# Odd mixer: pooled products around the gate matmuls, square roots two units later, forward scan into the kept sum, convolution ahead of the backward scan

## The reference, cut to what matters

```python
def odd_mixer(h, hc, w_in, pool_w, pool_scale, conv_w, conv_b, wa, ba, wx, bx, lam, need_ctx):
    z = h @ w_in
    ux, ug, up = jnp.split(z, CD_SPLITS, axis=-1)
    zc = hc @ w_in[:, :LRU_W]
    xl = depthwise_conv(ux, conv_w, conv_b, LRU_PAD)
    xc = depthwise_conv(zc[..., :LRU_W], conv_w, conv_b, LRU_PAD)
    h_lat = 0
    for d, reverse in enumerate((False, True)):
        # rglru_coeffs: r = sigmoid(u@wa + ba), gi = sigmoid(u@wx + bx), log_a = c * r
        #               a = exp(log_a), b = sqrt(1 - a^2) * gi * u
        a_c, b_c = rglru_coeffs(xc, wa[d], ba[d], wx[d], bx[d], lam[d])
        hs_c = linear_scan(a_c, b_c, 0, reverse)
        a_l, b_l = rglru_coeffs(xl, wa[d], ba[d], wx[d], bx[d], lam[d])
        h_lat = h_lat + linear_scan(a_l, b_l, hs_c[:, 0] if reverse else hs_c[:, -1], reverse)
    return [multiscale_pool(up, pool_w, pool_scale), h_lat * jax.nn.gelu(ug)]
```

## Time and profile before

| | us |
|---|---|
| median of 3 runs | 2664.08 |
| lowest, highest | 2663.63, 2664.1 |
| the profiled execution | 2664.78 |
| its span, first to last instruction | 2662.7 |
| TensorE busy in it | 2267.3 (85%) |
| odd mixer's units in the span, from L1873's first start to its last end | 1585.6 to 1848.5 |

### The profile page before, as it was taken

The page is one execution under the profiler, slowest core; times in us unless marked ns, Lnnn a source line. Parts: engine busy times, 40 slices in busy tenths (PEclk is TensorE's granted clock), DMA queues, the critical chain, the costliest instruction groups (busy, mean ns, idle before and its releaser), DMA issues. The chain is left out here.

```text
span 2662.7 us, 35013 instructions
## 1 busy us (share of the span) xinstructions
PE 2267.3 (85%) x15264; PEld 1086.8 (41%) x15264; DVE 729.2 (27%) x1158; ACT 607.1 (23%) x916; POOL 175.2 (7%) x126
## 2 busy tenths in 40 slices
PE   6498998987995699999999639888984999998874
PEld 3277886554443233333333224444433233332223
DVE  0422324653015211111111373444224111111104
ACT  2421012551004111111111143554013111111102
POOL 0001000000000000000000202241000000000002
PEclk8589999997997799999999759998996999999996
DMA  9600105305421889889999320001003999999985
GB/s 376 224 24 16 40 24 203 122 1 189 152 101 42 335 356 416 355 350 412 415 415 414 126 85 24 24 17 70 0 3 145 409 409 420 415 425 414 426 359 196
DMA packets 139500, 595.85 MB, mean 224 GB/s; under 512 B 25332, under 2 KB 52688, under 8 KB 114640
## 3 DMA queue, kind: packets, MB, share of 16 engines
q1 hardware_dynamic: 111824, 524.86, 49.3%
q0 software_dynamic: 11952, 43.52, 4.4%
q10 hardware_dynamic: 15568, 25.17, 2.7%
HBM read 534.79 MB, written 58.72 MB: 223 GB/s over the span
## 5 line engine op out<-in xcount | busy, mean ns | idle before, releaser
L1548 PE MATMUL ph<-w,x_t 128*32 128x512 f32 x6016 | 681.4, 606 | 39.9 <-DMA w<-in_exp_w 37.7
L1548 PEld LDWEIGHTS ph<-w,x_t 128*32 128x32 f32 x6016 | 190.5, 112 | 453.3 <-issue 428.4
L1561 PE MATMUL py<-w,g_t 128*32 128x512 f32 x3008 | 341.1, 594 | 1.0 <-DVE g_t L1667 1.0
L1661 DVE TENSOR_TENSOR hidden<-hidden,ph 64x512 f32<-64x512 f32 x94 | 101.9, 1084 | 768.4 <-ACT hidden L1619 768.4
L1166 PE MATMUL z<-Y,w_o 128*128 128x512 f32 (+1 forms) x640 | 255.5, 556 | 0.0
L1619 ACT ACTIVATE hidden<-ph 64x512 f32<-64x512 f32 x94 | 55.6, 592 | 695.7 <-PE ph L1548 695.7
L1873 PE MATMUL z<-hT,w_cd 128*128 128x512 f32 (+1 forms) x448 | 192.8, 590 | 4.9 <-ACT hT L477 4.9
L1561 PEld LDWEIGHTS py<-w,g_t 128*32 128x32 f32 x3008 | 93.6, 110 | 205.0 <-issue 203.7
L691 PE MATMUL z<-h_high,w_hi 128*128 128x512 f32 (+1 forms) x432 | 161.7, 374 | 15.3 <-DVE h_low L525 15.3
L1166 PEld LDWEIGHTS z<-Y,w_o 128*128 128x128 f32 x640 | 120.6, 192 | 128.7 <-issue 125.1
L1526 POOL DMA_INDIRECT x_rows<-h_tokens,index x47 | 44.4, 945 | 1843.0 <-PE px L1533 996.2
(11 more groups left out here) (293 smaller groups left out, 2104.0 us busy)
## 6 DMA issues: line engine op xcount, KB each, us to landing
w<-in_exp_w SPq DMA_DIRECT2D x192, 2048.0 KB, 15.7
ada_raw<-in_ada_w SPq DMA_DIRECT2D x24, 2048.0 KB, 17.9
y_slots<-y_rows ACTq DMA_DIRECT2D x188, 128.0 KB, 8.9
y_slots<-zero SPq DMA_DIRECT2D x29, 512.0 KB, 15.3
h_tokens<-h_rows SPq DMA_DIRECT2D x18, 512.0 KB, 2.6
w_ab<-in_w_in_ab SPq DMA_DIRECT2D x14, 512.0 KB, 3.9
w_cd<-in_w_in_cd SPq DMA_DIRECT2D x12, 512.0 KB, 3.9
x_t_saved<-xT SPq DMA_DIRECT2D x8, 640.0 KB, 8.1
```

What stands on the lines that cost most here:

```text
L1548: ins = pe.matmul(ph[row:row + UNIT, :], xt[:, k, at:at + UNIT], w13[:, place[2 * b + n] % RING, half, k, :], start=(k == 0), stop=(k == K ...
L1561: ins = pe.matmul(py[b % 2][row:row + UNIT, :], gt[:, k, n * UNIT:(n + 1) * UNIT], w2[:, place[2 * b + n] % RING, k, half * 512:(half + 1) ...
L1661: dve.tensor_tensor(hid[PAIR:P, :].rearrange("s (k q) -> s q k", k=FT), hid[0:PAIR, :].rearrange("s (q k) -> s q k", k=FT), ph[PAIR:P, :]. ...
```

## The change

It leaves every computation as it is and moves or redirects these:

1. **Pooled products.** Both now stand at one unit, ux i+1 c = 2 (for round 3: ug1 c = 0). After that unit's matmuls TensorE does the first pooled product, into the other bank (that of the unit before), then the second gates (rounds 0 to 2), then the second pooled product into this unit's bank. ScalarE scales both out directly after its copy of that unit.
2. **Second gates** after ux i+1 c = 2 instead of c = 1 (round 3: as before).
3. **Square roots** later: direction 0 at ux i+1 c = 1 instead of c = 0 (round 3: ug0 c = 1), direction 1 at up i+1 c = 1 instead of c = 0 (round 3: ug2 c = 0).
4. **Forward scan** over the latent tokens writes straight into `total[i]` and signals `s_fwd`; the sum adds the backward scan to it in place. `gate_out` of direction 0 waits for `s_fwd` in place of `s_sum`.
5. **Sigmoids**: `pxg` (into G) first, then `pa`; GpSimd's product waits for the first of them alone.
6. **Convolution** of round i ahead of `under_root` of the last round's direction 1.

```diff
             gates_at[place["up", i, 1]] = (i, 0)
-            gates_at[place["ux", i + 1, 1] if later else place["ug", 0, 1]] = (i, 1)
-            roots_at[place["ux", i + 1, 0] if later else place["ug", 0, 0]] = (i, 0)
-            roots_at[place["up", i + 1, 0] if later else place["ug", 1, 0]] = (i, 1)
-            for c in range(2):
-                pool_at[place["ux", i + 1, 1 + c] if later else place["ug", 1, c]] = (i, c)
+            gates_at[place["ux", i + 1, 2] if later else place["ug", 0, 1]] = (i, 1)
+            roots_at[place["ux", i + 1, 1] if later else place["ug", 0, 1]] = (i, 0)
+            roots_at[place["up", i + 1, 1] if later else place["ug", 2, 0]] = (i, 1)
+            n = place["ux", i + 1, 2] if later else place["ug", 1, 0]
+            pool_at[n] = i
+            pool_in[n - 1], pool_in[n] = 2 * i, 2 * i + 1
...
                     ins.then_inc(s_z, 1)
+                    if n in pool_at:
+                        pool_product(pool_at[n], 0, n - 1)
                     if n in gates_at:
                         gates(*gates_at[n])
                     if n in pool_at:
-                        pool_product(*pool_at[n], n)
+                        pool_product(pool_at[n], 1, n)
...
                     if i:
-                        act.wait_ge(s_sum, i)
-                    for gate, (dst, ps, name) in enumerate(((R, pa, "lru_ba"), (G, pxg, "lru_bx"))):
+                        act.wait_ge(s_sum if d else s_fwd, i)
+                    for gate, (dst, ps, name) in enumerate(((G, pxg, "lru_bx"), (R, pa, "lru_ba"))):
...
                     if n in pool_at:
-                        pool_out(*pool_at[n], n)
+                        pool_out(pool_at[n], 0, n - 1)
+                        pool_out(pool_at[n], 1, n)
...
-                    link.step(dve.tensor_tensor_scan(flip(G[:, lat]), flip(R[:, lat]), flip(S[:, lat]), first,
-                                                     ALU.mult, ALU.add))
+                    if d == 0:
+                        dve.tensor_tensor_scan(total[i], R[:, lat], S[:, lat], first, ALU.mult, ALU.add).then_inc(s_fwd, 1)
+                    else:
+                        link.step(dve.tensor_tensor_scan(flip(G[:, lat]), flip(R[:, lat]), flip(S[:, lat]), first,
+                                                         ALU.mult, ALU.add))
...
-                    dve.tensor_tensor(total[i], lanes[0][1][:, 0:SEQ], lanes[1][1][:, 0:SEQ], ALU.add).then_inc(s_sum, 1)
+                    dve.wait_ge(s_fwd, i + 1)
+                    dve.tensor_tensor(total[i], total[i], lanes[1][1][:, 0:SEQ], ALU.add).then_inc(s_sum, 1)
...
+                    conv(i)
                     if i:
                         under_root(i - 1, 1)
-                    conv(i)
-                    if i:
                         scans(i - 1, 1)
...
-                        pool.wait_ge(s_r, 2 * k + 2)
+                        pool.wait_ge(s_r, 2 * k + 1)
```

More of the change, by code:

```diff
@@ L1769, in odd_mixer @@
         place = {(kind, i, c): n for n, (m, i, kind, c) in enumerate(unit)}
-        gates_at, roots_at, pool_at = {}, {}, {}
+        gates_at, roots_at, pool_at, pool_in = {}, {}, {}, {}
         for i in range(BR):
@@ L1797, in odd_mixer @@
             s_w = [self.sem(ctx, f"o_w{i}") for i in range(NW)]
-            (s_sum, s_gw, s_pw, s_zero, s_z, s_ux, s_ug, s_up, s_cv, s_pg, s_r, s_a, s_q, s_sq, s_b, s_h, s_gu, s_y, s_pl, s_pd,
+            (s_sum, s_fwd, s_gw, s_pw, s_zero, s_z, s_ux, s_ug, s_up, s_cv, s_pg, s_r, s_a, s_q, s_sq, s_b, s_h, s_gu, s_y, s_pl, s_pd,
              s_pm, s_pe, s_ch) = (
-                self.sem(ctx, "o_" + n) for n in ("sum", "gw", "pw", "zero", "z", "ux", "ug", "up", "cv", "pg", "r", "a", "q", "sqr",
+                self.sem(ctx, "o_" + n) for n in ("sum", "fwd", "gw", "pw", "zero", "z", "ux", "ug", "up", "cv", "pg", "r", "a", "q", "sqr",
                                                   "b", "h", "gu", "y", "pl", "pd", "pm", "pe", "ch"))
@@ L1813, in wait_z_read @@
                     eng.wait_ge({"ug": s_ug, "up": s_up}[kind], 2 * i + c + 1)
-                if n in pool_at:
-                    of, half = pool_at[n]
-                    eng.wait_ge(s_pe, 2 * of + half + 1)
+                if n in pool_in:
+                    eng.wait_ge(s_pe, pool_in[n] + 1)
             @block.sync
```

## The result

The changed kernel's median is 2638.82 us (four runs, 2635.5 to 2642.04) beside 2663.86 for the kernel before (2661.9 to 2664.1): ratio 0.9908, 95% interval 0.989 to 0.9925, or 25.0 us. The forecast was 2643.5, 20.8 us saved by its sum. The profiled execution is the slowest of the four, 2642.04, with a span of 2640.0 (before: 2662.7).

What follows compares the result with a forecast made beforehand. TensorE, busy 85% of the span, was taken to bound the kernel, with 37.5 us lost in the odd mixer; 10.6 of waits and 6.1 of clock stay, so 20.8 saved: 2643.3, say 2643.5 us, range 2634 to 2651.

Steps and rivals of the forecast that it cites:

- The budget: TensorE in the odd mixer: 37.5 us lost above its work, 24.5 idle ahead of pooled products, 13.0 slow matmuls after waits.
- The copy's wait goes: Second pooled product, rounds 0 to 2: the 16.9 us of waits for ScalarE's copy and their clock cost go away.
- The convolution's room: Ahead of the next round's first gates: convolution needs 13.1 us, TensorE has 14.6 of work, so 1.5 us clear, no cost.
- GpSimd by turns: Pooling: GpSimd and VectorE wait for each other's instructions, so TensorE waits 4.0 us in round 1 and 4.7 in round 2.
- rival by form: GpSimd's later passes take 3.05 us whatever VectorE does; waits 0.1 and 3.6, 28.5 us saved, 2635.6 us; chance 0.18.
- rival without collision: GpSimd's and VectorE's turns fall otherwise: no wait in rounds 1 and 2, 2.6 to 4 us left, 2630; chance 0.07.
- Round 2's wait: TensorE waits 4.7 us for GpSimd's pooling ahead of the second gates, with one pass more than round 1.
- round 3's: Waits ahead of round 3's two pooled products, for GpSimd (0.5 us) and for the copy of ug1 c = 0: together 1.9.
- Round 1's wait: TensorE waits 4.0 us for GpSimd's pooling ahead of the second gates, with the subtraction done at 25.4 us.
- Clock: Slow matmuls behind waits: 2.7 us each in rounds 1 and 2 (2.4 to 3.0), 0.7 in round 3; 6.1 in all.
- In sum: Mixer: 10.6 us of waits and 6.1 of clock stay, 16.7 against 37.5, so 20.8 us saved.
- The rule on the shared ports: Whole-instruction lock: VectorE's product in round 2 would wait for GpSimd's scaling, some 1.6 us more, 2645.

Runs made afterwards that it cites:

- the fastest kernel: Changed kernel with both pooled products behind the second gates and round 3's products one unit later, at ug1 c = 1: mixer 190.8 us, median 2627.4 us.
- the convolution second: Changed kernel with the convolution put back behind under_root of the last round's direction 1: mixer 214.3 us, median 2652.6 us, ratio 0.9934 to 0.9965.
- the places alone: Kernel before with only the new places of pooled products and second gates: mixer 221.2 us, median 2659.4 us, ratio 0.998 to 1.0002.
- short under_root: Changed kernel with VectorE's two under_root instructions writing 8 columns, not 1283 (values wrong): mixer 197.3 us, median 2634.9 us.
- sigmoids as before: Changed kernel with the sigmoid of R first and GpSimd's product after both sigmoids: mixer 208.0 us, median 2647.3 us, ratio 0.9924 to 0.9951.
- forward scan as before: Changed kernel with the forward scan into the lane and the first sigmoid behind the sum again: mixer 214.0 us, median 2653.2 us.
- roots as before: Changed kernel with the square roots at their old units: mixer 202.9 us, median 2641.3 us, ratio 0.9903 to 0.994.

## Why the prediction was right, point by point

- **The budget.** 37.5 us of losses, 24.5 in waits: the fastest kernel has won 35.7 of it.
- **The copy's wait goes.** As told. The copy of the 256-token unit started 0.18 us after the root and 0.2 after the unit's end, in round 0 of both traces of the changed kernel.
- **The convolution's room.** 1.5 forecast, 1.2 measured. The two kernels with `under_root` ahead show what it is worth: waits of 4.39 us (the convolution second) and 4.46 (the places alone) in each of three rounds.
- **GpSimd by turns.** Right, and the step that decides: product 4.57 (4.8 forecast), sum 3.75 (3.8), a wait in round 1 and in round 2, none in round 0. The rival by form is refuted by short under_root; the rival without collision by the 4.57.
- **Round 2's wait** was 4.68 against 4.7, **round 3's** 1.68 against 1.9.
- **Round 1's wait was mis-sized**: 2.26 against 4.0. The step was the last turn. I let VectorE's product, released by the root at 21.5, go ahead of the subtraction and hold it until 23.0. GpSimd was 0.6 us faster through the passes and scaling than I had it, its subtraction began at 1682.96, and VectorE's product at 1683.08: 0.12 us decided that VectorE waited (3.57 for 1.50) and not GpSimd. In the edit with the sigmoids as before VectorE's product was 0.09 us ahead (1684.59 and 1684.68), GpSimd's edges lost 1.6 us to it, and the wait was 4.68.
- **Clock was mis-sized**: 1.8 us behind each of the two long waits, where I took 2.7 (range 2.4 to 3.0), and about 0.2 in round 3, where I took 0.7. The same kernel again had 1.8 and 2.3. My range came from the waits of 6.29 and 3.89 us. The trace of before had a third, of 4.33 us in round 2, near in length to the 4.68, and behind it product and units cost 1.8 us (1761.23 to 1777.60, 16.37 for 14.59):

```profile
1761.23 1.14 PE L1859 MATMUL z<-pool,pool_weights 128*128 128x512 f32 x2 [4.33 <-ACT u_pad L1930]
1762.17 15.59 PE L1873 MATMUL z<-hT,w_cd 128*128 128x512 f32 x32
1777.60 2.31 PE L1848 MATMUL pa<-x_conv,gate_w 128*128 128x512 f32 x6
```

- **In sum** 16.7 us were to stay and 13.2 did: 1.7 from round 1's turn, 1.8 from the clock behind the long waits, the rest from small terms that cancel. The mixer won 24.4 us, the medians 25.0.
- **The rule on the shared ports.** The Trainium skill, SBUF — State Buffer, "Who interferes with whom", has the engine that issues first hold the ports that VectorE and GpSimd share for its whole instruction. The traces agree for two-input instructions (4.57, 3.75, 3.57) and not for GpSimd's scaling. In round 2 of the changed kernel VectorE's product ran its solo 1.50 in the middle of it; VectorE's timeline:

```profile
1728.54 1.50 DVE L1983 TENSOR_TENSOR lru<-lru 128x1283 f32<-128x1283 f32 x1 [3.38 <-ACT lru L1920]
```

GpSimd's scaling there is 1727.02 to 1729.79, in the fence above. By the rule the product would have waited 1.2 us for it. The scaling held VectorE only at its start: in round 3 VectorE's context scan, asked for at 1778.63 when the scaling had just got its turn, took 1.41 for 0.69 and was done at 1780.04, and the scaling ran on to 1781.22.

## What to carry to other kernels

When a wait is removed, work out the next chain up to the same instruction, with its room in us, before counting the gain: here the mixer's 24 us hung on several parts, and the one that moved the large wait was worth some 5 alone. In a stream that is taken in order, put what waits for the slowest helper behind work that waits for nothing; two lines moved past the gates gave 9 to 10 us more. And where VectorE and GpSimd both read two operands, place them by turns in the schedule, since a lead of 0.1 us decided here whether VectorE lost 2.1 us or GpSimd 1.6.

## What the runs showed of the hardware that I had not expected

What a wait costs TensorE in clock is not given by its length. A wait of 4.39 us cost 1.5, 1.8 and 2.8 us in three rounds of one execution (the first three matmuls, `pa`, took 3.83, 4.07 and 4.64 for 2.31 in the rows of the convolution second; the granted clock over the gates was 0.75, 0.72 and 0.62), one of 4.46 cost 2.4, 2.9 and 2.5 in the places alone (its first gates from 1666.92 to 1673.58, 6.66 for 4.30), one of 4.68 cost 1.8 and its like in two other traces 2.3 and 1.5, one of 4.43 (forward scan as before, round 3) 3.3, one of 7.48 only 2.0, one of 2.26 and one of 2.02 (short under_root) 1.8, and those of 1.94 and 1.96 ahead of round 3's second product 1.7. One of 2.65 and one of 2.60 cost only 0.1, the latter in TensorE's timeline of the roots as before:

```profile
1687.29 1.13 PE L1859 MATMUL z<-pool,pool_weights 128*128 128x512 f32 x2 [2.60 <-POOL pool L2046]
1688.25 2.31 PE L1848 MATMUL pa<-x_conv,gate_w 128*128 128x512 f32 x6
...
1692.55 1.02 PE L1859 MATMUL z<-pool,pool_weights 128*128 128x512 f32 x2
```

(1687.29 to 1692.55 is 5.26 for 5.16, and the granted clock there is 1.00.) What sets it I did not test; a range of 0.1 to 3.3 us behind any wait of 1.9 us or more is what these rows allow.
